# Six of the 22 tile pairs of the FFN's upward projection formed by seven half-size products in place of eight

## The reference

```
D_FF = 2816; FFN_CONV = 3
def causal_dwconv(x, w): ...            # y[t] = w[2] x[t] + w[1] x[t-1] + w[0] x[t-2], per channel
def conv_ffn(h, w_up, conv_w, w_down):  # h 512x1024, w_up 1024x5632, w_down 2816x1024
    gu = causal_dwconv(h @ w_up, conv_w)
    g, u = jnp.split(gu, 2, axis=-1)
    return (jax.nn.silu(g) * u) @ w_down
x = x + conv_ffn(rmsnorm(x, norm_ffn_gain), ffn_w_up, ffn_conv_w, ffn_w_down)
```

## Time and profile before

| | |
|---|---|
| median of three executions | 1222.37 us |
| the profiled execution: its own time, its span | 1223.61 us, 1221.5 us |
| PE busy, instructions | 1207.6 us (99%), 6667 |
| POOL busy | 700.3 us (57%), 538 |
| DVE busy | 698.6 us (57%), 1239 |
| ACT busy | 612.0 us (50%), 1184 |
| low parts of weights by POOL, 128x512 | 1369 ns in the mean, 384 of them |
| share of the chain that ended last: PE, DVE, ACT, POOL | 95%, 3%, 1%, 1% |
| clock of PE granted | 1.00 |

### The profile page before, as it was taken

How to read it: one execution, slowest core, us unless ns; L and a number is a source line. 1 busy time by engine, 2 the same in 40 slices (tenths; PEclk the granted TensorE clock), 3 DMA queues, 4 the chain that set the end, 5 groups by cost and what they waited for, 6 DMA issues and landing times.

```text
span 1221.5 us, 18340 instructions
## 1 busy us (share of the span) xinstructions
PE 1207.6 (99%) x6667; PEld 990.1 (81%) x6667; DVE 698.6 (57%) x1239; ACT 612.0 (50%) x1184; POOL 700.3 (57%) x538
## 2 busy tenths in 40 slices
PE   9999999999999999999999999999999999999997
PEld 7977777777888899987887777878888888889886
DVE  5545426757646777745697555445454545966224
ACT  6355535676644344445634656544444444333544
POOL 8673232353269776855484566545655565886842
PEclk9999999999999999999999999999999999999999
DMA  7432222122223333354142223333333333333332
GB/s 236 107 95 73 70 61 61 52 63 77 70 62 103 95 98 94 107 179 116 52 119 58 58 62 96 96 85 104 87 88 102 103 88 80 101 96 117 108 87 69
DMA packets 62432, 112.22 MB, mean 92 GB/s; under 512 B 6856, under 2 KB 11464, under 8 KB 62344
## 3 DMA queue, kind: packets, MB, share of 16 engines
q1 hardware_dynamic: 62200, 111.06, 32.5%
q10 hardware_dynamic: 144, 0.00, 0.0%
HBM read 108.87 MB, written 2.16 MB: 91 GB/s over the span
## 4 chain that ended last, share of the span: by engine, by line
PE 95%; DVE 3%; ACT 1%; issue 1%; POOL 1%; DMA 0%; SPq 0%; DVEq 0%; POOLq 0%; ACTq 0%
PE pb L1101 23%; PE pb L1102 23%; PE pb L1104 23%; PE pb L1154 3%; PE pb L1156 3%; PE pb L1155 3%; PE pb L1310 2%; PE pb L1286 2%; PE pb L1163 2%; PE pb L1253 1%; PE pb L1224 1%; PE pb L1226 1%; PE pb L1225 1%; PE pb L1207 1%; PE pb L1205 1%; PE pb L1275 1%
## 5 line engine op out<-in xcount | busy, mean ns | idle before, releaser
L2684 POOL TENSOR_TENSOR wlo<-raw,whi 128x512 fp32r<-128x512 f32 (+2 forms) x384 | 518.7, 1369 | 333.2 <-ACT whi L1503 332.2
L1101 PE MATMUL pb<-HH,whi 128*128 128x512 f32 x856 | 345.4, 404 | 0.0
L1102 PE MATMUL pb<-HL,whi 128*128 128x512 f32 x856 | 338.5, 395 | 0.0
L1104 PE MATMUL pb<-HH,wlo 128*128 128x512 f32 x856 | 337.5, 394 | 0.0
L1503 ACT ACTIVATE whi<-raw 128x512 fp32r<-128x512 f32 (+2 forms) x384 | 226.1, 613 | 106.9 <-PE pb L1104 55.7
L1101 PEld LDWEIGHTS pb<-HH,whi 128*128 128x128 f32 x856 | 161.3, 188 | 42.2 <-issue 4.6
L1102 PEld LDWEIGHTS pb<-HL,whi 128*128 128x128 f32 x856 | 161.0, 188 | 38.1 <-issue 2.9
L1104 PEld LDWEIGHTS pb<-HH,wlo 128*128 128x128 f32 x856 | 160.9, 188 | 37.4
L1976 DVE TENSOR_TENSOR pb<-pb,rff 128x512 f32<-128x512 f32 x44 | 30.8, 700 | 124.0 <-PE pb L1104 117.6
L1621 ACT ACTIVATE P<-P,stat 128x256 f32<-128x256 f32 (+3 forms) x96 | 50.5, 527 | 78.7 <-DVE stat L2246 57.1
L2684 POOL TENSOR_TENSOR fl<-cv,fh 128x512 fp32r<-128x512 f32 x22 | 28.9, 1314 | 86.4 <-ACT fh L1897 86.4
(11 more groups left out here) (461 smaller groups left out, 2512.2 us busy)
## 6 DMA issues: line engine op xcount, KB each, us to landing
raw<-in_wall SPq DMA_DIRECT2D x368, 256.0 KB, 2.8
raw<-in_wall SPq DMA_DIRECT2D x8, 260.0 KB, 3.2
X<-in_xT SPq DMA_DIRECT2D x8, 256.0 KB, 5.4
X<-in_xT SPq DMA_DIRECT2D x2, 1024.0 KB, 7.6
outT<-PP SPq DMA_DIRECT2D x8, 256.0 KB, 2.5
raw<-in_wall SPq DMA_DIRECT2D x10, 192.0 KB, 2.4
raw<-in_wall SPq DMA_DIRECT2D x9, 128.0 KB, 2.4
cst<-in_cst SPq DMA_DIRECT2D x1, 832.0 KB, 7.6
```

Of the source, the lines that this page charges most:

```text
L1101: pe.do.matmul(b, hi, xh[k], start=start, stop=False, skip_group_check=tile[0] == "down")
L1102: pe.do.matmul(b, hi, xl[k], start=False, stop=False, skip_group_check=tile[0] == "down")
L1104: m = pe.do.matmul(b, lo, xh[k], start=False, stop=stop, skip_group_check=tile[0] == "down")
L2684: g.do.tensor_tensor(lo, x, hi.bitcast(F32), ALU.subtract).then_inc(*up(name, point))
```

## The change

Tile pairs j = 5, 7, 9, 11, 13, 15 of the upward projection (`UPS`) are formed by seven products with 256 columns each, 84 matmuls in place of 48 of 512 columns. A11 and A12 are of half 0's tile, A21 and A22 of half 1's. The input sums (`TSU`, with high and low parts `THU`, `TLU`; `tus`, `tuh`, `tul` in the rows) are made in tile pairs 1 to 3, and those of the last block (kp = 3) are split behind half 0's product of tile pair 4: for each of the four blocks ACT makes three copies with the gain, DVE four differences of 256 columns, ACT one copy of 128x1024 and POOL two low parts. For a pair the plan gives up the separate products and takes three banks ("ffn" 0, "cd", "ffn" 1). During the seven products ACT copies a half bank to `u` (`v0`) and DVE makes `u2` from it (behind S2), four sums behind S3 and one behind S4 (`product_up`, all with 256 columns and a PSUM operand). Product A12 waits for `u2`. The low parts of all factors, S3's too, are made by POOL. `taps(1, j-1)` and `product(j-1)` move behind S3, `product(j-2)` moves ahead of `scaled(1, j-1)`, and both `scaled` of j stand behind the pair. For A22 and S2 the look-ahead splits are issued behind S2.

```diff
 NGATE = len(PAIRS)
+UPS = (5, 7, 9, 11, 13, 15)
+NUP = NGATE + len(UPS)
...
     def pair(self, p):
...
         for x in FACTORS:
-            self.split_to(self.unit_of[p, x] + LOOK)
+            if not NGATE <= p < NUP or x not in ("A22", "S2"):
+                self.split_to(self.unit_of[p, x] + LOOK)
             self.add("product7", p, x)
+            if NGATE <= p < NUP and x == "S2":
+                self.split_to(self.unit_of[p, x] + LOOK)
+            if x == "S3" and NGATE <= p < NUP:
+                self.add("taps", 1, UPS[p - NGATE] - 1)
+                self.add("product", UPS[p - NGATE] - 1)
...
+        sums_of, parts_of = {(j, 0): j - 1 for j in range(1, 5)}, {(j, 1): j - 1 for j in range(1, 4)}
+        sums_of[3, 1], parts_of[4, 0] = sums_of.pop((4, 0)), 3
         for j in range(NPAIR):
+            if j in UPS:
+                for t in (("ffn", 0, j), ("cd", j), ("ffn", 1, j)):
+                    take(t)
+                self.pair(NGATE + UPS.index(j))
             for half in range(2):
-                take(("ffn", half, j))
-                self.proj(("ffn", half, j), "ffn_up", 2816 * half + P * j)
+                if j not in UPS:
+                    take(("ffn", half, j))
+                    self.proj(("ffn", half, j), "ffn_up", 2816 * half + P * j)
...
+                if half and j + 1 in UPS and j not in UPS:
+                    add("product", j - 1)
                 add("scaled", half, j)
-                if (half, j) != (0, 0):
-                    add("taps", 1 - half, j - 1 + half)
                 if half:
+                    add("taps", 0, j)
                     add("swish", j)
-                elif j:
-                    add("product", j - 1)
+                elif j and j not in UPS:
+                    add("taps", 1, j - 1)
+                    if j + 1 not in UPS:
+                        add("product", j - 1)
+                if (j, half) in parts_of:
+                    add("t_parts", 3, parts_of[j, half])
+                if (j, half) in sums_of:
+                    for i in range(2):
+                        take(("ts", sums_of[j, half], i))
+                    add("t_sums", 3, sums_of[j, half])
...
# PE, product7
+                if kind(p) == "up":
...
+                    if x == "A12":
+                        pe.wait_ge(*at("u2", p))
...
# ACT, t_sums
+                    a.do.activation(TSU[kp][:, 0:T], xk[kp], ACT.Copy, scale=gain).then_inc(*up("a_t7"))
+                    a.do.activation(ps("ts", kp, 0)[:, H:T], xk[kp][:, H:T], ACT.Copy, scale=gain).then_inc(*up("a_t7"))
+                    a.do.activation(ps("ts", kp, 1), xk[kp + 4], ACT.Copy, scale=vecs("ffn_norm", kp + 4)).then_inc(
...
# ACT, product7
+                if kind(p) == "up" and x == "S2":
+                    a.wait_ge(*at("product7", p, x))
+                    a.wait_ge(*at("u3", p - 1))
+                    a.do.activation(U7, ps("ffn", 0, UPS[p - NGATE])[:, 0:H], ACT.Copy).then_inc(*up("a_c7", ("v0", p)))
...
# DVE
-                elif x == "A12":
+                elif x == "A12" and kind(p) != "up":
                     w = plan.unit_of[p, "S3"]
...
+            def product_up(p, x):
+                j, left, right = UPS[p - NGATE], slice(0, H), slice(H, T)
+                ab, cd, e = ps("ffn", 0, j), ps("cd", j), ps("ffn", 1, j)
...
+                if x == "S2":
...
+                    plus(U7, ab[:, right], U7, ("u2", p))
+                elif x == "S3":
...
+                    plus(W8, cd[:, left], U7)
+                    plus(ZU, cd[:, right], U7, ("u3", p))
...
+                    plus(e[:, right], cd[:, right], W8, ("empty", ("cd", j)))
+                    plus(e[:, left], e[:, left], ZU)
+                elif x == "S4":
...
+                    plus(ab[:, right], ab[:, right], W8)
...
# POOL, low part of a factor
-                elif factor[1] == "S3":
+                elif factor[1] == "S3" and kind(factor[0]) != "up":
                     return
```

More of the change, by code:

```diff
@@ L948, in sums_at, with kind @@
             return S7 if p < NGATE else S8
+        def kind(p):
+            return "gate" if p < NGATE else "up" if p < NUP else "down"
         T_AT = {"S1": 0, "S3": 1, "A22": 2, "S2": 3}
@@ L1004, in build @@
         ffn_work = a3.p
+        sums_places = [(ffn_work, ffn_work + 8 * T)] + [(place[f"fh{j}"], place[f"fl{j}"]) for j in (16, 18, 20)]
+        THU, TLU = ([tensor_at(f"tu{n}{kp}", [P, 2 * T], F32R, sums_places[kp][x]) [:, :] for kp in range(4)]
+                    for x, n in enumerate("hl"))
+        TSU = [tensor_at(f"tus{kp}", [P, 2 * T], F32, sums_places[kp][1])[:, :] for kp in range(4)]
+        ZU = tensor_at("zu", [P, H], F32, 226176)[:, :]
         a3.p += 4 * (4 * T + 64)
@@ L1117, in product7 @@
                 later = []
-                if p < NGATE:
+                if kind(p) == "up":
+                    g, (xhs, xls), (ths, tls), j = 3, (hh, hl), (THU, TLU), UPS[p - NGATE]
+                    tile, half = {"A11": (("ffn", 0, j), 0), "S2": (("ffn", 0, j), 1), "S1": (("cd", j), 0), "S3": (("cd", j), 1),
+                                  "A12": (("ffn", 0, j), 0), "S4": (("ffn", 0, j), 1), "A22": (("ffn", 1, j), 0)}[x]
+                    b, starts = ps(*tile)[:, H * half:H * half + H], x in ("A11", "S1", "A22", "S4")
+                    if x == "A12":
+                        pe.wait_ge(*at("u2", p))
+                    elif x in ("A11", "S1", "A22"):
+                        free(tile)
+                elif p < NGATE:
                     g, (xhs, xls), (ths, tls) = 0, (hh, hl), (TH7, TL7)
@@ L2051, in step @@
                     v.do.tensor_tensor(dst, one, two, op).then_inc(*up("v_t7", *points))
+                if g == 3:
+                    left, right = slice(0, H), slice(H, T)
+                    one, two = (ps("ts", kp, i) for i in range(2))
+                    v.wait_ge(*at("t_scaled", kp))
+                    step(x11, one[:, right], x11, ALU.subtract, ("empty", ("ts", kp, 0)))
+                    step(x12, two[:, right], x12, ALU.subtract)
+                    v.wait_ge(*last("v_t7"))
+                    step(x22, two[:, right], x11, ALU.subtract)
+                    v.wait_ge(*last("v_t7"))
+                    step(x21, two[:, left], x22, ALU.subtract, ("t_raw", g, kp), ("empty", ("ts", kp, 1)))
+                    return
+                xhs, xls = ((hh, hl), (FH, FL))[g]
                 if g:
@@ L2593, in scaled @@
                 b = ps("ffn", half, j)
-                v.wait_ge(*at("full", ("ffn", half, j)))
+                if j in UPS:
+                    v.wait_ge(*last("v_c7"))
+                else:
+                    v.wait_ge(*at("full", ("ffn", half, j)))
                 v.wait_ge(*at("rff"))
```

63 lines of the change are left out of this document (46 added, 17 removed).

## The result

The changed kernel takes 1234.22 us (median of five, 1233.97 to 1234.96) against 1222.41 us: ratio 1.0096, 95% interval 1.0084 to 1.0108, 11.8 us slower. The profiled executions differ by 10.6 us in their own time and by 10.9 in their span (1232.4 against 1221.5). The forecast was 1233 us. The profiled execution before lay 1.2 us above its median and the one after at its median, which is the difference between 11.8 and 10.6.

What follows compares the result with a forecast made beforehand. PE bounds the kernel before; after the change DVE, with ACT and POOL in its chain, was to bound the rounds. Terms: -7.5 + 11.7 (five rounds) + 6.5 (first pair) = +10.7 us, forecast 1233 us, range 1224 to 1241.

Steps and rivals of the forecast that it cites:

- PE gives back 7.5 us: Six upward pairs at 9.90 us in place of 11.16 save 7.5 us; PE's round becomes 21.06 us.
- DVE's meetings with POOL, 4.6 us a round: Eight DVE operations with two SBUF operands each lose 0.58 us to POOL per round; bounds 0 and 7.3.
- Hand-offs, 2.5 us a round: DVE waits 1.7 us before `u2` and 0.8 us for ACT's scaled-bank copy each round; bounds 0.5 and 3.5.
- The round, 23.4 us: Seven-product pair plus ordinary pair: DVE needs 16.3 + 4.6 + 2.5 us; PE waits 2.3 us, 11.7 over five rounds.
- The first pair, 6.5 us: First seven-product pair: PE waits 4.2 us in A22 for late low parts, plus 2.3 us for A12 and S4.
- the A12 and S4 chain of this pair adds its 2.3: In the first pair, PE also waits 2.3 us for the low parts of A12 and S4.
- Who releases PE: In every pair PE idles before the low-part matmuls of A12 and S4 until POOL releases it.
- PE as the bound: Rival: meetings and hand-offs take under 4.8 us a round, PE never waits there; 1217.5 to 1219.1 us, chance 0.09.
- rarer meetings: Rival: mean meeting cost of 0.35 us in place of 0.58, round 21.6 us; 1222 to 1225 us, chance 0.17.
- more frequent ones: Rival: mean DVE-POOL meeting cost of 0.75 us, round 24.8 us; 19 us slower, 1241 us, chance 0.12.
- POOL as the bound: Rival: POOL's 13 operations and eight delays set the round, but need 19.9 us, 1.2 below PE's; no chance given.
- The signs: Profile after: `cv<-cv,cv` and sums at 1.2 us mean, up to 1.8; taps, `scaled` unchanged; POOL's low parts sometimes 1.75.

Runs made afterwards that it cites:

- e6: Changed kernel with POOL's low parts of weights and products in the upward loop made as one-operand copies, the subtraction left out: 1220.34 us, ratio 0.9983.
- e8: Changed kernel, all six pairs, with tanh and swish in PSUM, tanh issued behind the copy to `u`, input sums made earlier: 1218.72 us, ratio 0.9969.
- e7: Changed kernel with four pairs (6, 9, 12, 15), tanh and swish in PSUM, tanh behind the copy to `u`, input sums moved: 1217.17 us, ratio 0.9956.
- e3: Changed kernel with tanh and swish written into half 0's PSUM bank in place of SBUF: 1224.41 us, ratio 1.0015.
- e2: Changed kernel with the tanh of the preceding tile's half 0 issued behind ACT's copy to `u` instead of in front: 1228.81 us, ratio 1.0052.
- e5: Changed kernel with the input sums and their parts made earlier: 1230.33 us, ratio 1.0066.
- e4: Changed kernel with S3's low part in the six upward pairs made by DVE in place of POOL: 1233.83 us, ratio 1.0093.

## Why the prediction was right, and where it was not

- *PE gives back 7.5 us*: right. Without waits the rounds are 20.87 to 20.99 us in e6 and e8 (21.06 predicted), and e7's four pairs gave 5.2 us.
- *DVE's meetings with POOL, 4.6 us a round*: right in sum. The sums' excess over 0.69 us is 1.14 (`s8c`), 0.98, 0.82 and 0.57, together 3.5, and four `cv<-cv,cv` have 0.31 each, 1.2: 4.7 us. I had spread it evenly, 0.58 us for each of the eight; in this loop the sums bear three quarters of it. That the total came out owes something to luck, for in e3 the same four sums have an excess of 1.9 us together. e3 shows the cause for swish and product. For the sums no run changes an operand; the ends of both engines' operations, 0.55 us apart in all 34 meetings, show it, and e6 agrees, though only together with POOL's shorter operations.
- *Hand-offs, 2.5 us a round*: 1.55 and 0.64, 2.2 us. e2 takes one away and gains 1.0 a round, which shows that it stood in the path.
- *The round, 23.4 us*: 23.2 in three of five and 24.16 in the one behind the first pair. Waits of the second to the sixth pair: 24.16 + 23.20 + 23.24 + 23.26 - 4 x 21.06 = 9.6, and 12.04 - 9.90 = 2.1 in the last, together 11.7 us, as predicted.
- *The first pair, 6.5 us*: 17.12 - 9.90 = 7.2, but made up otherwise. The wait in A22 is 4.7 us by the starts (4.2 predicted). The predicted chain was added up wrongly: its terms give 7.0 us and not 6.7, so a wait of 4.5, and without the two delays of 0.45 they give 3.6 and not the lower bound of 2.6. The 2.3 us of waits in A12 and S4 that I added are not there. DVE and POOL had caught up while PE stood and then ran slowly, which e5_place bears out: without the long wait both waits are there. In their place stand 2.5 us that PE lost at the lower clock. Right in size by luck: the step "the A12 and S4 chain of this pair adds its 2.3" failed, and the clock was no term of mine: it stood at nothing, and measured 2.5 us.
- *Who releases PE*: POOL's low parts of A12 and S4, as predicted, once S4's wait is read beside POOL's timeline.
- Together -7.5 + 11.7 + 7.2 = +11.4; the loop itself begins 0.8 us earlier in this profiled execution, which leaves +10.6 for 10.9 in the span. That offset lies in stages that the change doesn't touch. The loop begins between 787.3 and 789.2 us in the profiled executions of all these kernels, at 788.56 before and at 787.78 after, so it is of the size of their scatter. No run was made for it.
- *Rivals*: PE as the bound (rounds of 21.06 us), rarer meetings (21.6) and more frequent ones (24.8) are out by the round's 23.2. POOL as the bound is out by e4, where POOL has one operation less and the round stays, and by e3, where POOL has the same operations and the round is shorter.
- *The signs*: `cv<-cv,cv` has a mean of 1.0 us, not 1.2, and the sums 1.26 to 1.83; taps and `scaled` are unchanged, and POOL's second value is there (1.44 to 1.76 us).

Open: whether the round would be PE's if the sums alone met nothing, with swish and product as they are. A sum of two weights has no operand in PSUM to begin with, and it wasn't tried.

## What to carry to other kernels

Work taken from a saturated engine pays only as far as the next engine's chain, counted with its waits in that new round: here an engine at 50% of its time before became the bound by some 5 us of new operations, 5 of meetings and 2 of hand-offs in each round. Two cheap edits brought much of the 11.8 us back, each by itself: an intermediate placed in PSUM so that VectorE's operation has one SBUF operand (9.8 us), and a short copy issued ahead of an activation that waits (5.4 us). And the number of tiles treated is a knob. Four pairs took 1217.17 us and six 1218.72, and only the four ran without a wait; the two kernels also make their input sums at other places, so the number alone isn't shown to be the reason.

## What the hardware showed

- A VectorE operation of 128x512 with two SBUF operands took 0.69 us alone. One that started beside a GpSimd operation (1.3 us) ended 0.55 us behind the end of that operation, up to 1.84 us in the rows shown. With one operand in PSUM it stayed at 0.69. GpSimd's copy with a single operand (0.62 us) held it up as well (1.00), which I had not expected.
- A wait of PE of 4.7 us brought its granted clock to 0.50, the 1.2 GHz level, and PE then worked at it for 5.5 us; this cost 2.5 us more, half as much again. It came back in e2, e4 and e6 (waits of 3.9 to 4.5 us by the idle time before the matmul), and in e3 behind 3.95 us, where it cost 1.6. In e5, waits of 1.9 us and less left the clock at 1.00. No run has a wait between 1.9 and 3.9 us.
- The meetings depend on how the two engines' operations fall beside each other: the sum `s8c` had means of 1834, 1273 and 1702 ns in the kernel after, e3 and e7.
